# Combining the samples' tile of a mixture of experts in four quarters on the array, and summing it in quarters

## The reference

```python
h = rmsnorm(x, g_ffn) * (1 + sc2) + sh2
p = softmax(h @ w_router + b_router); top 4 of 32, gates renormalised
z = h @ w_gu[e] + b_gu[e]                      # 1024 -> 2048
a = clamped_swiglu(z)                          # 1024
y[row] += gate[row, e] * (a @ w_dn[e] + b_dn[e])
x = x + gt2 * y                                # gt2: one row of 1024 per prompt or sample
```

## Time and profile before

| | |
|---|---|
| median of 3 runs | 1533.03 us (1530.78 to 1534.72) |
| profiled execution | 1533.65 us, of which span 1531.8 us |
| TensorE / VectorE / ScalarE / GpSimd busy | 95% / 44% / 21% / 5% of the span |
| granted TensorE clock, mean | 0.974 |
| expert weights | 32 x 12.58 MB |
| one expert in the steady loop | 29.75 us |

### The profile page before, as it was taken

The page is one execution under the profiler, slowest core; times in us unless marked ns, Lnnn a source line. Parts: engine busy times, 40 slices in busy tenths (PEclk is TensorE's granted clock), DMA queues, the critical chain, the costliest instruction groups (busy, mean ns, idle before and its releaser), DMA issues. The chain is left out here.

```text
span 1531.8 us, 21636 instructions
## 1 busy us (share of the span) xinstructions
PE 1461.4 (95%) x8310; PEld 673.9 (44%) x8310; DVE 680.1 (44%) x1626; ACT 317.5 (21%) x591; POOL 84.2 (5%) x123
## 2 busy tenths in 40 slices
PE   4999999999899889999999999999999999999997
PEld 2457677777777443333333333333333333333332
DVE  1264333367775534453353344335334433533444
ACT  3013131245551121111111111111111111111110
POOL 1300000222202100000000000000000000000001
PEclk9999899999999979999999999999999999999998
DMA  9775734353323849999999999999999999999991
GB/s 340 240 282 195 283 149 131 126 181 139 138 111 115 321 166 409 424 424 417 425 424 417 426 426 421 421 424 424 418 428 424 424 419 427 423 420 426 422 422 53
DMA packets 65299, 501.84 MB, mean 328 GB/s; under 512 B 6352, under 2 KB 12292, under 8 KB 40407
## 3 DMA queue, kind: packets, MB, share of 16 engines
q1 hardware_dynamic: 54960, 463.07, 73.6%
q0 software_dynamic: 10288, 38.08, 7.2%
HBM read 495.56 MB, written 9.15 MB: 329 GB/s over the span
## 5 line engine op out<-in xcount | busy, mean ns | idle before, releaser
L1123 PE MATMUL bank_v<-arena 128*64 128x512 f32 (+16 forms) x4848 | 840.3, 475 | 28.4 <-DMA arena<-in_w_ada 10.0
L1123 PEld LDWEIGHTS bank_v<-arena 128*64 128x64 f32 (+8 forms) x4848 | 343.6, 139 | 485.6 <-issue 393.0
L1123 PE MATMUL bank_s<-arena 128*64 128x512 f32 (+3 forms) x1936 | 474.6, 558 | 0.8 <-DVE arena L852 0.8
L1123 PEld LDWEIGHTS bank_s<-arena 128*64 128x64 f32 (+3 forms) x1936 | 178.3, 150 | 248.9 <-issue 217.7
L922 DVE TENSOR_SCALAR arena<-bank_v 128x512 f32<-128x512 f32 x32 | 22.1, 691 | 391.6 <-PE bank_v L1123 391.6
L936 DVE TENSOR_TENSOR arena<-bank_v,arena 128x512 f32<-128x512 f32 (+1 forms) x192 | 123.4, 682 | 150.6 <-PE bank_v L1123 150.6
L941 DVE TENSOR_TENSOR x_rows<-x_rows,arena 128x512 f32<-128x512 f32 (+1 forms) x192 | 123.8, 684 | 3.3
L1019 ACT ACTIVATE arena<-arena 128x512 f32<-128x512 f32 x32 | 20.1, 630 | 426.2 <-DVE arena L922 426.2
L1127 PEld LDWEIGHTS bank_s<-const_tables,arena 128*128 128x128 f32 (+4 forms) x619 | 74.8, 168 | 76.0 <-issue 37.5
L1127 PE MATMUL bank_s<-const_tables,arena 128*128 128x128 f32 (+4 forms) x619 | 97.9, 290 | 10.1 <-issue 3.0
L1635 DVE TENSOR_TENSOR arena<-bank_v,arena 128x288 f32<-128x288 f32 (+9 forms) x128 | 49.5, 387 | 100.5 <-PE bank_v L1123 73.1
(11 more groups left out here) (113 smaller groups left out, 617.3 us busy)
## 6 DMA issues: line engine op xcount, KB each, us to landing
arena<-in_w_gu SPq DMA_DIRECT2D x128, 2048.0 KB, 11.9
arena<-in_w_dn SPq DMA_DIRECT2D x64, 2048.0 KB, 9.4
arena<-in_w_ada SPq DMA_DIRECT2D x12, 2048.0 KB, 11.3
arena<-in_w_in SPq DMA_DIRECT2D x10, 2048.0 KB, 12.8
arena<-in_state_win_kv POOLq DMA_DIRECT2D x8, 512.0 KB, 6.9
arena<-in_w_out SPq DMA_DIRECT2D x2, 2048.0 KB, 21.1
out_win_sample<-in_state_win_kv POOLq DMA_DIRECT2D x1, 4064.0 KB, 27.5
x_rows<-in_x_prompt POOLq DMA_DIRECT2D x4, 512.0 KB, 9.1
```

The lines of the kernel that those rows point to most:

```text
L1123: return pe.matmul(out, l, r, start=first, stop=last)
```

## The change

The combine of the samples' tile (i = 2) becomes four matmuls of 256 columns. Quarter c holds the channels `(c // 2) * 512 + (c % 2) * 256` and on; its operands are on row half c // 2 of the array, and its output goes to partitions 32c to 32c + 31 of one bank (bank 2). The samples' rows of `x` and of the gate are kept in the same form, 128 partitions by 256 columns (`xq`, `gate2q`), until the end. VectorE's part for this tile becomes one product and one sum on 128 x 256. Before the loop, four copies bring `x` into the form, and the gate comes by four transfers beside the prompt's one. At the end the samples' result is stored in four transfers instead of two.

```diff
+        gate2q, xq = (arena[:, shift2.offset + D + n * 256:shift2.offset + D + (n + 1) * 256] for n in range(2))
+        SAMPLE_QUARTERS = [(32 * c, c // 2, (c % 2) * 256) for c in range(4)]
...
             def combine(bank, i):
                 o, n = TILES[i]
+                if i == 2:
+                    for p0, half, c0 in SAMPLE_QUARTERS:
+                        hp = slice(half * CAP, (half + 1) * CAP)
+                        last = mm(ebank(bank)[p0:p0 + 32, 0:256], GT[hp, o:o + n], yb[hp, c0:c0 + 256], True, True)
+                    return last
                 for half in range(2):
...
             rows2(0)
+            for p0, half, c0 in SAMPLE_QUARTERS:
+                copy(xq[p0:p0 + 32, :], x[0:32, 2, half * 512 + c0:half * 512 + c0 + 256])
             for t_ in (yb, GT, ohx):
...
                     ve.wait_ge(sem("sum_filled"), 3 * e + i + 1)
+                    if i == 2:
+                        ve.tensor_tensor(cb[:, 0, 0:256], ebank(2)[:, 0:256], gate2q, mul).then_inc(sem("sum_drained"), 1)
+                        ve.wait_ge(sem("sum_drained"), 3 * e + i + 2)
+                        ve.tensor_tensor(xq, xq, cb[:, 0, 0:256], add).then_inc(sem("sum_added"), 1)
+                        ve.wait_ge(sem("sum_added"), 3 * e + i + 1)
+                        continue
...
-            ve.wait_ge(sem("gate2_rows"), 32)
+            ve.wait_ge(sem("gate2_rows"), 16 * 5)
...
+            tt(fin[:, 1, 512:], fin[:, 1, 512:], x[:, 1, 512:], add, "y_rows_late")
+            ve.wait_ge(sem("tail_filled"), 3)
+            tt(fin[:, 2, 0:256], ebank(4)[:, 0:256], gate2q, mul)
+            tt(fin[:, 2, 0:256], fin[:, 2, 0:256], xq, add, "y_rows_late")
...
-            mod_rows(gate2, 5, "gate2_rows")
+            dma(gate2[:, 0, :], bc(mod_dram[0, 5 * D:6 * D], P), "gate2_rows")
+            for p0, half, c0 in SAMPLE_QUARTERS:
+                c = 5 * D + half * 512 + c0
+                dma(gate2q[p0:p0 + 32, :], mod_dram[1:1 + DB * DT, c:c + 256], "gate2_rows")
...
+            sp.wait_ge(sem("y_rows_late"), 2)
+            for p0, half, c0 in SAMPLE_QUARTERS:
+                c = half * 512 + c0
+                sp.dma_start(y_sample.rearrange("b t d -> (b t) d")[:, c:c + 256], fin[p0:p0 + 32, 2, 0:256]).then_inc(sem("output_stored"), 16)
+            sp.wait_ge(sem("output_stored"), 16 * 8)
```

More of the change, by code:

```diff
@@ L958, in ve_late @@
             barrier(ve, "ve")
-            for i, (o, n) in enumerate(TILES):
+            for i, (o, n) in enumerate(TILES[0:2]):
                 ve.wait_ge(sem("tail_filled"), i + 1)
@@ L962, in ve_late @@
                     hs = slice(half * 512, half * 512 + 512)
[L963 to L967, removed]
+                    tt(fin[0:n, i, hs], ebank(2 * i + half)[0:n, :], gate2[0:n, 0, hs], mul, "y_gated")
+            tt(fin[:, 1, 512:], fin[:, 1, 512:], x[:, 1, 512:], add, "y_rows_late")
+            ve.wait_ge(sem("tail_filled"), 3)
+            tt(fin[:, 2, 0:256], ebank(4)[:, 0:256], gate2q, mul)
+            tt(fin[:, 2, 0:256], fin[:, 2, 0:256], xq, add, "y_rows_late")
             barrier(ve, "ve")
@@ L1053, in pool_late @@
             pool.wait_ge(sem("v_filled"), tags["v"].index(("router", 1)) + 1)
-            mod_rows(gate2, 5, "gate2_rows")
+            dma(gate2[:, 0, :], bc(mod_dram[0, 5 * D:6 * D], P), "gate2_rows")
+            for p0, half, c0 in SAMPLE_QUARTERS:
+                c = 5 * D + half * 512 + c0
+                dma(gate2q[p0:p0 + 32, :], mod_dram[1:1 + DB * DT, c:c + 256], "gate2_rows")
             barrier(pool, "pool")
[L1056 to L1063, removed]
+            for i, half in ((0, 0), (0, 1), (1, 0)):
+                hs = slice(half * 512, half * 512 + 512)
+                pool.wait_ge(sem("y_gated"), 2 * i + half + 1)
+                pool.tensor_tensor(fin[:, i, hs], fin[:, i, hs], x[:, i, hs], ALU.add).then_inc(sem("y_rows"), 1)
             barrier(pool, "pool")
@@ L1106, in sp_late @@
             barrier(sp, "sp")
[L1107 to L1116, removed]
+            for i, half in ((0, 0), (0, 1), (1, 0), (1, 1)):
+                o, n = TILES[i]
+                hs = slice(half * 512, half * 512 + 512)
+                if (i, half) == (1, 1):
+                    sp.wait_ge(sem("y_rows_late"), 1)
+                else:
+                    sp.wait_ge(sem("y_rows"), 2 * i + half + 1)
+                sp.dma_start(y_prompt[0][o:o + n, hs], fin[0:n, i, hs]).then_inc(sem("output_stored"), 16)
+            sp.wait_ge(sem("y_rows_late"), 2)
[3 more added lines that the diff above has]
+            sp.wait_ge(sem("output_stored"), 16 * 8)
             barrier(sp, "sp")
```

## The result

The changed kernel took 1516.82 us in the median of its first four executions (1515.97 to 1519.97), the kernel before 1533.88. The ratio is 0.9884 with a 95% interval of 0.9843 to 0.9925. Two further comparisons of the same two kernels gave 0.9928 (0.9900 to 0.9957) and 0.9912 (0.9881 to 0.9943). Over all executions the medians are 1520.37 us (19 executions, 1512.78 to 1528.68) and 1534.99 us (48 executions, 1524.16 to 1542.58). So the change is a gain of some 14 us, a little under 1%. The forecast was 12.5 us and a time of 1520.8 in a range from 1517.8 to 1525.7. The first median missed the range by 1.0 us at its lower end. The profiled execution took 1519.97 us, its span 1518.2.

What follows compares the result with a forecast made beforehand. The prediction took TensorE's instruction stream to bound the expert loop. A gain of 12.8 us there less 0.3 us in the tail made 12.5 us, giving 1520.8 us, in a range of 1517.8 to 1525.7 us.

Steps and rivals of the forecast that it cites:

- TensorE's instruction stream is the bound: In the expert loop, TensorE's issuing, not the DMA, was said to set the 29.75 us per expert.
- The combine's slot: Samples' combine on TensorE in the expert loop: 0.97 to 0.57 us, saving 0.40 us per expert, 12.8 us over 32.
- The Trainium skill's rule against two row tiles in one PSUM bank: At the samples' combine, row halves sharing one bank would take turns, leaving the slot at 0.97 us; kept as a rival, 0.08.
- VectorE costed at nothing: In the loop, VectorE loses 1.85 us of work per expert but is idle 60% of it, so the gain counts nothing.
- The DMA pays out of its margin: For the last expert's w_gu loads, the 12.2 us prefetch margin was said to cover TensorE's 12.4 us earlier need: cost 0.
- Rival A: DMA takes over near the loop's end: 29.90 us per expert, a 4.9 us stall, 1522 to 1525.7 us; chance 0.12.
- Set-up at nothing: Before the loop, four copies of 0.9 to 1.7 us in all and three more gate transfers were said to cost nothing.
- The tail 0.3 us longer, at most 0.8: After the last expert, four sample stores instead of two end 0.3 us later, bounds -0.2 and +0.8 us.
- the upper bound's case: In the tail, each small sample store takes 0.5 us to issue and the next waits: 0.8 us longer.
- The sum: Whole kernel: 12.8 us gained in the loop less 0.3 us in the tail, 12.5 us.
- The range: Whole kernel's measured time: 1517.8 to 1525.7 us, taking in rival A and median scatter of a microsecond or two.
- the likeliest case: Whole kernel with the forecast holding: 1519.0 us (0.43 us per expert, tail -0.2) to 1523.7 us (0.31 us); chance 0.76.

## Why the prediction was right or wrong

- *TensorE's instruction stream is the bound.* Right. The period fell by what was taken from the stream (0.41 us), and rose and fell with the slot in every experiment (1.84, 0.57, 0.35 us: periods 30.61, 29.34, 29.12), until the DMA's floor. I read one wait of TensorE in the loop that is no issue time; the view has a second, for VectorE's products of the combine. It is the same after the change, so the sum does not need it:

```profile
PEld bank_v L1123 <- DVE arena L936: 25.2, 31, 0.8
```

```profile
PEld bank_v L1140 <- DVE arena L951: 25.2, 31, 0.8
```

- *The combine's slot: 0.97 to 0.57, 0.40 us, 32 times.* Right; 0.40 in the slot and 0.41 in the period. The extra cost of 0.03 us was there as taken: 0.43 + 0.14, where it was 0.86 + 0.11. My choice of 0.03 between 0 and 0.12 had no row of its own.
- *The Trainium skill's rule against two row tiles in one PSUM bank* (TensorEngine Tiling (Array Packing), Restrictions and Gotchas). The trace disagrees for this placement: with two banks instead of one the slot is the same 0.57 us. No run had two row halves in one bank at the same column place.
- *VectorE costed at nothing.* Wrong by 0.43 us. It is idle in the loop, but after the last expert all engines meet, and VectorE was the last to come. I looked for who waits for it inside the period only. In the loop VectorE gave back 1.71 us per expert (11.91 to 10.20), not 1.85: I had added four instructions that overlap.
- *The DMA pays out of its margin.* Right that TensorE never waits; wrong in the size. I took 424 GB/s for what the stream can do, but that was what TensorE asked for (12.58 MB in 29.75 us). Its floor is 29.36 us, so landing times grew from 13.8 to 15.0 us at most where I forecast 21 to 24. In the other two traces of this kernel they grew from 13.4 to 16.0 and from 13.9 to 15.4. Rival A needed a stream of 29.90 us and had no ground.
- *Set-up at nothing.* Right. The four copies took 1.25 us and VectorE's idle time shrank from 4.01 to 2.78 us; the distance of the loop's first issue from the w_gu issue ahead of it is 26.87 us in both profiles. *The tail 0.3 us longer, at most 0.8.* At full clock it is 0.73 us longer (10.15 to 10.88 us from the first combine to the end): the four sample stores go 0.48 us apart, 1514.46 to 1515.90, the upper bound's case.
- *The sum.* 32 x 0.41 = 13.1, and 0.43 at the barrier, less 0.73 in the tail, is 12.8 us, against 13.0 between the traces with a full-clock tail (961.11 and 948.11). With the half-clock tail of the profiled execution it is 13.8. The forecast of 12.5 was small by a few tenths, and that is partly luck: the 0.43 us at the barrier, which I put at nothing, and the 0.43 us that the tail cost above my 0.3 cancel.
- *The range.* This is the step that failed. I let the medians scatter by a microsecond or two. The changed kernel's 19 executions have a standard deviation of 4.8 us, so a median of four may well lie 3 us off: of all sets of four out of the 19, 29% have a median 3 us or more from 1520.37, and 13% one below 1517.8. The first median lay 3.6 us below that of all 19, which is 0.4 us from the forecast. In the traces the scatter sits ahead of the loop, where the rows of one execution could not show it; the three executions of before, 1530.78 to 1534.72, hinted at it. Of the first four executions only the slowest, 1519.97, left a trace. That the other three began their loops earlier, near 566 to 567 us if their loop and tail were 948.2 too, is inferred; it lies within the 564.22 to 577.43 of the twelve traces. One slip beside it: the ends of the likeliest case, 1519.0 and 1523.7, were counted from two bases, 1533.03 and 1533.3. From one base they move by 0.3 us, which changes nothing.

## What to carry to other kernels

When an f32 matmul leaves places of the array empty, cut its columns and put the parts side by side: the streaming time divides by the places, and the shape change stays (here 0.14 us in the slot, 0.24 us with its neighbours). When two resources both read as full, find which one sets the rate before taking that rate as the other's limit; here the DMA's own floor was 0.4 us per expert below the rate it ran at. Compare kernels from a marker behind the noisy part, such as the loop's first issue, which here turned a scatter of 13 us into one of 0.1 among the traces after the change, and look at the clock of the tail apart: it is worth 1 us.

## What the runs showed of the hardware

- Four f32 matmuls of 64 by 32 on four column places run at once, with two row halves in one bank, with two banks, or all on one row half: 0.57 us for eight records of 256 columns each time, and 1.84 us at one place. Leaving the four out of a stream of 128 by 64 matmuls saves 0.67 us, so the shape change costs 0.24 us beside the 0.43 of streaming.
- The weight stream of 2 MB loads has a floor of 29.36 us per 12.58 MB. At 0.02 us under it the longest landing times rose by 1.2 to 2.6 us in 30 experts (three traces), at 0.24 us under it by 7.7 us, at 0.69 us under it by 11 us in 17 experts, and then TensorE waited. In the kernel before, 0.39 us above it, they rose by 0.2 and 0.7 us.
- A sum of 128 by 256 on VectorE took 0.42 us alone and 0.91 and 1.48 us while GpSimd summed on its own side; a product of that size out of a bank took 0.42 us beside GpSimd too.
- Kernels that do not differ ahead of the loop start it between 564 and 577 us, with 61 us at half clock ahead of it in the earliest and 92 us in the latest.
